# The sample tile projected from unsplit f32 weights in two column groups, with the splits of the output weights begun a quarter sooner

## The reference, cut to what matters

```python
y = jnp.concatenate([o_gla * silu(gg), o_pool * silu(pg), o_fox * silu(fg)], axis=-1) @ wo
return h + rmsnorm(y, post)
```

## Time and profile before

| | |
|---|---|
| median of 3 runs | 701.57 us (701.45 to 702.39) |
| the profiled execution, own time | 700.78 us |
| its span | 699.1 us |
| TensorE busy | 658.0 us, 94% |
| VectorE, ScalarE, GpSimd busy | 56%, 37%, 20% |

### The profile page before, as it was taken

How to read it: one execution, slowest core, us unless ns; L and a number is a source line. 1 busy time by engine, 2 the same in 40 slices (tenths; PEclk the granted TensorE clock), 3 DMA queues, 4 the chain that set the end, 5 groups by cost and what they waited for, 6 DMA issues and landing times.

```text
span 699.1 us, 13106 instructions
## 1 busy us (share of the span) xinstructions
PE 658.0 (94%) x5120; PEld 565.0 (81%) x5120; DVE 393.3 (56%) x706; ACT 262.1 (37%) x480; POOL 142.9 (20%) x162
## 2 busy tenths in 40 slices
PE   2999999999999999999999989989999997999996
PEld 2799999898999889999999955766576655688885
DVE  4824926672455305169999965444433559345543
ACT  6637344111111346122121155645574566231321
POOL 4034112111111011233312040222222103112210
PEclk9999999999999999999999999999999999999999
DMA  8411103131100032352210381667676512033232
GB/s 248 124 38 49 43 1 75 29 94 31 32 26 8 4 84 97 98 166 77 61 31 1 119 272 42 179 180 209 186 226 176 207 37 100 9 98 106 75 122 90
DMA packets 60759, 67.29 MB, mean 96 GB/s; under 512 B 15188, under 2 KB 50907, under 8 KB 60697
## 3 DMA queue, kind: packets, MB, share of 16 engines
q1 hardware_dynamic: 55529, 51.37, 24.9%
q0 software_dynamic: 5168, 15.08, 7.3%
HBM read 57.71 MB, written 8.68 MB: 95 GB/s over the span
## 4 chain that ended last, share of the span: by engine, by line
PE 82%; DVE 9%; ACT 4%; issue 2%; SPq 1%; DMA 1%; DVEq 0%
PE PS L1764 14%; PE PS L1765 13%; PE PS L1766 13%; PE PS L1693 5%; PE PS L1692 5%; PE PS L1694 5%; PE PS L2053 3%; PE PS L2035 3%; PE PS L1988 3%; PE PS L2010 2%; PE PS L1953 2%; PE PS L1940 2%; DVE rows_odd L1576 2%; DVE YF L1455 1%; DVE wol_a L1598 1%
## 5 line engine op out<-in xcount | busy, mean ns | idle before, releaser
L1764 PE MATMUL PS<-xh,wh 128*128 128x368 f32 x576 | 196.1, 340 | 0.3 <-DVE RA L1392 0.3
L1765 PE MATMUL PS<-xl,wh 128*128 128x368 f32 x576 | 190.2, 330 | 0.0
L1766 PE MATMUL PS<-xh,wl 128*128 128x368 f32 x576 | 189.8, 329 | 0.0
L582 POOL TENSOR_TENSOR wl<-wr,wh 128x1024 fp32r<-128x1024 f32 x24 | 61.5, 2560 | 292.0 <-ACT wh L944 291.7
L1764 PEld LDWEIGHTS PS<-xh,wh 128*128 128x128 f32 x576 | 108.2, 188 | 4.4 <-issue 1.8
L1765 PEld LDWEIGHTS PS<-xl,wh 128*128 128x128 f32 x576 | 108.2, 188 | 0.9
L1766 PEld LDWEIGHTS PS<-xh,wl 128*128 128x128 f32 x576 | 108.2, 188 | 0.0
L1264 DVE TENSOR_TENSOR wr<-wr,small 128x1024 f32<-128x1024 f32 (+1 forms) x26 | 37.1, 1426 | 43.3 <-DMA wr<-in_w_in_dram 43.2
L1692 PE MATMUL PS<-woh,yh 128*128 128x512 f32 (+1 forms) x144 | 56.1, 390 | 0.6 <-DVE wol_b L1598 0.6
L1435 DVE RECIPROCAL RA<-RA 128x1104 f32<-128x1104 f32 x8 | 56.4, 7053 | 0.3
L1694 PE MATMUL PS<-woh,yl 128*128 128x512 f32 (+1 forms) x144 | 56.0, 389 | 0.0
(11 more groups left out here) (305 smaller groups left out, 1084.2 us busy)
## 6 DMA issues: line engine op xcount, KB each, us to landing
wr<-in_w_in_dram SPq DMA_DIRECT2D x24, 512.0 KB, 3.7
kpage<-in_cache_fox_k_dram SPq DMA_DIRECT2D x64, 192.0 KB, 2.7
RA<-in_cache_fox_v_dram POOLq DMA_DIRECT2D x32, 192.0 KB, 3.7
pagesB<-in_cache_fox_v_dram POOLq DMA_DIRECT2D x32, 192.0 KB, 3.6
YF<-in_x_prompt_dram SPq DMA_DIRECT2D x8, 512.0 KB, 6.8
xres<-in_x_prompt_dram SPq DMA_DIRECT2D x8, 512.0 KB, 3.9
out_y_p_dram<-zout SPq DMA_DIRECT2D x16, 256.0 KB, 2.1
wo_raw_a<-in_w_out_dram SPq DMA_DIRECT2D x6, 512.0 KB, 4.8
```

The lines of the kernel that those rows point to most:

```text
L582: eng.tensor_tensor(low, wr[:, c % 2, :, 0:m], wh[:, c % 2, :, 0:m].bitcast(F32), ALU.subtract).then_inc(wlo_done, 1)
L1764: pe.matmul(out, high, xh[:, k, cols], start=(k == 0), stop=False)
L1765: pe.matmul(out, high, xl[:, k, cols], start=False, stop=False)
L1766: ins = pe.matmul(out, low, xh[:, k, cols], start=False, stop=(k == KT - 1))
```

## The change

Five edits, which go together:

- The sample tile is projected from the unsplit weights with plain f32 matmuls: for each k-block two matmuls of 64 stationary columns and 512 moving ones, the first into PSUM partitions 0 to 63 of the slot's first bank, the second into partitions 64 to 127 of its second bank. 16 matmuls in place of 48. Its Y is no longer split (one piece of work less for ScalarE and for GpSimd).
- The raw blocks 0 to 5 must live longer, so the low parts 0 to 5 have a place of their own, over `QK`, which is free once the last scores are made. Blocks 6 and 7 are still overwritten by their low parts: the sample tile uses them first, and VectorE's X 6 waits for that (`sample_late`).
- In the order, the sample tile moves from behind the last sum to behind the products of (2,3,0) and (2,3,1), and its "E" to behind the turned tile (2,3,4), ahead of the last product and sum.
- W 0 to 2 move from the quarter (2,2) to (2,1), and the others follow sooner; `wo_high(0)` waits for the keys of the last sequence to be used instead of its values, `wo_high(3)` for its turned probabilities. X 0 to 3 stand together behind the exponentials of (2,2).
- `rooms` is 2 for the quarter (2,2): all scores of the last quarter are made in its first part, and both "M" of tiles 6 and 7 stand in its second.

```diff
-        rooms = max(1, len(units) - 1 - after)
+        rooms = 2 if (p, q) == (2, 2) else max(1, len(units) - 1 - after)
...
-TAIL = {(2, 2, 0): [("W", 0), ("W", 1)], (2, 2, 1): [("X", 0), ("W", 2)],
-        (2, 2, 2): [("X", 1), ("X", 2), ("W", 3)], (2, 2, 3): [("X", 3), ("W", 4), ("Y", SAMPLE)],
-        (2, 3, 0): [("X", 4), ("W", 5), ("Y", FIRST)], (2, 3, 1): [("X", 5)], (2, 3, 2): [("W", 6)],
-        (2, 3, 3): [("X", 6), ("W", 7)], (2, 3, 4): [("X", 7)]}
+TAIL = {(2, 1, 1): [("W", 0), ("W", 1), ("W", 2)], (2, 2, 1): [("W", 3), ("W", 4), ("W", 5)],
+        (2, 2, 3): [("X", 0), ("X", 1), ("X", 2), ("X", 3)], (2, 3, 1): [("X", 4), ("X", 5), ("W", 6), ("Y", FIRST)],
+        (2, 3, 3): [("W", 7), ("S", SAMPLE), ("X", 6), ("X", 7)], (2, 3, 4): [("E", SAMPLE)]}
...
+        def out_part(user, half):
+            r = slice(NS * half, NS * half + NS) if user[1] == NTILE else slice(0, P)
+            return s_head(user, half)[r, :]
...
             def wo_high(k):
                 if k == 0:
-                    drained(act, ("s_attend", NB - 1))
+                    drained(act, ("s_scores", NB - 1, 2))
+                elif k == 3:
+                    drained(act, ("s_probsT", NB - 1, 1))
...
             def wo_low(k):
+                if k == 0:
+                    s_ready(dve, P1S[-1])
+                elif k == 6:
+                    dve.wait_ge(sample_late, 1)
                 dve.wait_ge(wohi_done, k + 1)
...
             def project_out(user):
                 t = user[1]
                 s_taken(pe, user)
+                if t == NTILE:
+                    drained(pe, ("s_outT", NB - 1))
+                    late_first = [6, 7, 0, 1, 2, 3, 4, 5]
+                    for k in late_first:
+                        pe.wait_ge(d_wo[k], 16)
+                        y = Y[:, k, ycol(t):ycol(t) + NS]
+                        lower = pe.matmul(out_part(user, 0), y, wo_raw[k][:, 0:D // 2], start=(k == 6),
+                                          stop=(k == 5), skip_group_check=True)
+                        upper = pe.matmul(out_part(user, 1), y, wo_raw[k][:, D // 2:D], start=(k == 6),
+                                          stop=(k == 5), skip_group_check=True)
+                        if k == 7:
+                            upper.then_inc(sample_late, 1)
+                    lower.then_inc(out_half, 1)
+                    upper.then_inc(s_full, 1)
+                    return
```

More of the change, by code:

```diff
@@ L216, in plan @@
     order += [("V", unit) for unit in behind] + [("R", ("sum",) + behind[0][:2])]
-    for n, t in enumerate(PROJ):
+    for n, t in enumerate(PROJ[1:], 1):
         if n >= 2:
-            order.append(("Y", ("proj", t)))
-        if n:
-            order.append(("E", ("proj", PROJ[n - 1])))
+            order += [("Y", ("proj", t)), ("E", ("proj", PROJ[n - 1]))]
         order.append(("S", ("proj", t)))
@@ L243, in slot_of @@
     return SF[user] % 2
+OUT_USERS = [k for k in SUSERS if k[0] == "proj"]
+OUT_OF_SLOT = {k: sum(slot_of(o) == slot_of(k) for o in OUT_USERS[:i + 1]) for i, k in enumerate(OUT_USERS)}
 P1S = [k for k in SUSERS if k[0] == "P1"]
@@ L261, in sem, with stage @@
             return ctx.enter_context(nc.semaphore(name))
+        def stage(*tensors):
+            with ExitStack() as s:
+                return [s.enter_context(nc.sbuf_tensor(n, d, t)) for n, d, t in tensors]
+        _, wol_a = stage(("pad_y", [P, 8 * NT], F32), ("wol_a", [P, 6, D], F32R))
         YF = sb("YF", [P, 14 * NT])
@@ L306, in build @@
         PS = ctx.enter_context(nc.psum_tensor("PS", [P, 8, 512], F32))
-        def stage(*tensors):
-            with ExitStack() as s:
-                return [s.enter_context(nc.sbuf_tensor(n, d, t)) for n, d, t in tensors]
         region_a = ("RA", [P, 6 * NT], F32)
@@ L322, in build @@
             ("rows_odd", [P, 2 * (score_width(6) + score_width(7))], F32))
-        wol_a, _, yh0, yl0, yh1, yl1, xres, zout, woh, wol_b, gpost = stage(
-            ("wol_a", [P, 6, D], F32R), ("pad_a", [P, 6 * NT - 6 * D], F32),
-            ("yh0", [P, KT, P], F32R), ("yl0", [P, KT, P], F32R), ("yh1", [P, KT, P], F32R),
+        _, yh0, yl0, yh1, yl1, xres, zout, woh, wol_b, gpost = stage(
+            ("pad_a", [P, 6 * NT], F32), ("yh0", [P, KT, P], F32R), ("yl0", [P, KT, P], F32R), ("yh1", [P, KT, P], F32R),
             ("yl1", [P, KT, P], F32R), ("xres", [P, D], F32), ("zout", [P, D], F32),
@@ L429, in build @@
         out_half, half_squared = sem("out_half"), sem("half_squared")
+        sample_late = sem("sample_late")
         def place(key):
@@ L495, in s_emptied @@
         def s_emptied(eng, user):
-            eng.wait_ge(s_free[slot_of(user)], PROJ.index(user[1]) // 2 + 1)
+            eng.wait_ge(s_free[slot_of(user)], OUT_OF_SLOT[user])
         def s_ready(eng, user):
@@ L887, in _ @@
                     load_bias(2)
-            for n_, t in enumerate(PROJ):
+            for n_, t in enumerate(PROJ[1:]):
                 g.wait_ge(yhi_done, n_ + 1)
-                m = P if t < NTILE else NS
-                g.tensor_tensor(yl[n_ % 2][:, :, 0:m], Y[:, :, ycol(t):ycol(t) + m], yh[n_ % 2][:, :, 0:m].bitcast(F32),
+                g.tensor_tensor(yl[n_ % 2][:, :, :], Y[:, :, ycol(t):ycol(t) + P], yh[n_ % 2][:, :, :].bitcast(F32),
                                 ALU.subtract).then_inc(ylo_done, 1)
@@ L1140, in squares_out @@
                     act.wait_ge(d_y, 32 * n_)
-                act.activation(zout[0:m, low], s_slot(user)[0:m, low], ACT.Square, accum_out=zhalf[0:m, 0:1]
+                act.activation(zout[0:m, low], out_part(user, 0), ACT.Square, accum_out=zhalf[0:m, 0:1]
                                ).then_inc(half_squared, 1)
@@ L1145, in squares_out @@
                 s_ready(act, user)
-                act.activation(zout[0:m, high], s_slot(user)[0:m, high], ACT.Square, accum_out=zstat[0:m, 0:1]
+                act.activation(zout[0:m, high], out_part(user, 1), ACT.Square, accum_out=zstat[0:m, 0:1]
                                ).then_inc(half_squared, 1)
@@ L1161, in y_high @@
             def y_high(n_):
[L1163 to L1168, removed]
+                t = PROJ[1 + n_]
+                drained(act, ("sum", 2, t // 2))
                 if n_ >= 2:
-                    s_ready(act, ("proj", PROJ[n_ - 2]))
-                act.activation(yh[n_ % 2][:, :, 0:m], Y[:, :, ycol(t):ycol(t) + m], ACT.Copy).then_inc(yhi_done, 1)
+                    s_ready(act, ("proj", PROJ[n_ - 1]))
+                act.activation(yh[n_ % 2][:, :, :], Y[:, :, ycol(t):ycol(t) + P], ACT.Copy).then_inc(yhi_done, 1)
             for kind, key in PLAN:
                 if kind == "Y":
-                    y_high(PROJ.index(key[1]))
+                    y_high(PROJ.index(key[1]) - 1)
                 elif kind == "W":
@@ L1609, in finish @@
                     dve.wait_ge(half_squared, 2 * n_ + n_half + 1)
-                    ins = dve.tensor_tensor(zout[0:m, cols], s_slot(user)[0:m, cols], gpost[0:m, cols], ALU.mult)
+                    r = slice(NS, 2 * NS) if t == NTILE and n_half else slice(0, m)
+                    ins = dve.tensor_tensor(zout[0:m, cols], out_part(user, n_half), gpost[r, cols], ALU.mult)
                 ins.then_inc(s_free[slot_of(user)], 1)
@@ L2080, in project_out @@
                     cols = slice(512 * half, 512 * half + 512)
-                    ins = product(out[0:m, cols], lambda k: (yh[n_ % 2][:, k, 0:m], yl[n_ % 2][:, k, 0:m]),
+                    ins = product(out[:, cols], lambda k: (yh[n_ % 2][:, k, :], yl[n_ % 2][:, k, :]),
                                   lambda k: (woh[:, k, cols], wol[k][:, cols]))
```

3 lines of the change are left out of this document (1 added, 2 removed).

## The result

**The times.** The changed kernel takes 697.29 us, the median of eight executions (696.65 to 699.66), against 702.37 us (701.35 to 704.55), the median of eight of the kernel before: ratio 0.9931, 95% interval 0.9915 to 0.9947. That is 0.69% faster, some 4.8 us. The forecast was 696.8 us, within 695.6 to 699.4. Its profiled execution has an own time of 696.65 us and a span of 695.0.

The account below looks back on a forecast made before the run. TensorE, busy 94% of the span, was taken as the bound, with idle time at 560 to 605. First full tile at 600.1 instead of 604.93 gives -4.8 us against the median 701.57: 696.8 us, range 695.6 to 699.4.

Parts of the forecast that it names:

- The sum: Whole kernel: first full tile at 600.1 instead of 604.93, so span and time fall by 4.8 us.
- A, the sample tile: Sample tile's projection on TensorE: eight f32 pairs at 0.90 us take 7.2 us instead of 11.11, -3.9 us.
- B, three early high parts: ScalarE's queue at (2,1): W 0 to 2 delay the cached values to 564.86, +1.1 us of TensorE idle.
- C, the last scores: Quarter (2,2): tile's maximum at 576.7 instead of 578.78; TensorE waits 0.5 us for exponentials instead of 2.41.
- D, VectorE: Low parts and copies: X 0 to 3 until 584.35, copy until 586.5 (+0.7); products of (2,3) start at 587.5 as before.
- E, the hand-over: Values to first full tile: sample tile until 596.6, new wait for its PSUM slot, first full tile at 600.1, -4.8 us.
- The step that was wrong: Eight full tiles after the sample tile: no gap, so the end moves by as much as the first full tile.
- rival 1: Tail: clock falls to 1.2 GHz over values and sample tile, +1.7 us, 698.5; chance 0.13.
- rivals 2 and 3: Sample tile's f32 pairs: groups don't overlap, 704.0 us, chance 0.04; or weight loads show, 701.0 us, chance 0.03.
- rival 4: ScalarE: the early high parts' 2.94 us passes on whole instead of 1.1, +1.8 us, 698.6; chance 0.10.

Follow-up runs that it names:

- one_group: The changed kernel with both halves of the sample tile in PSUM partitions 0 to 63, one column group: 703.74 us, ratio 1.0022 to the kernel before.
- w_late: The changed kernel with high parts W 0 to 2 moved back to quarter (2,2), beside W 3 to 5: 698.00 us, ratio 0.9932 to the kernel before.
- before_qk: The kernel before with only low parts 0 to 5 placed over QK and X 0 moved right ahead of X 1: 703.59 us, ratio 1.0017.
- rooms_old_2: The changed kernel with the old spreading of the last scores (rooms as before), run again for a second profile: 702.02 us, once.
- x0_early: The changed kernel with X 0 alone moved ahead of VectorE's copy of (2,2,3): 696.44 us, ratio 0.9912 to the kernel before.
- rooms_old: The changed kernel with the old spreading of the last scores (rooms as before): 701.44 us, ratio 0.9970 to the kernel before.
- again_before: The kernel before, unchanged, run once more for a second profile: 700.80 us, once.

## Why the prediction was right

By its own steps. Positions are those of after's own profile, whose head is 0.43 us longer than the one that the forecast counted from. So where a position up to the sample tile agrees with the forecast as it stands, it came 0.43 us sooner than forecast when counted from R, and the close agreement is in part luck:

- **The sum.** Forecast -4.8 us, and the ratio gives -4.8. Between the profiles it is -5.76 to the first full tile, +1.2 in the full tiles, +0.43 in the head, -4.1 in all. The forecast was 0.93 too cautious up to the first full tile (it had 604.93 - 600.1 = 4.83): 0.43 ahead of the sample tile, 0.23 in it and 0.27 behind it. And it was blind to the 1.2 behind. The two misses nearly cancel, so the total is better than its parts, by luck.
- **A, the sample tile.** 7.2 us forecast, 6.97 measured (589.40 to 596.37): a pair of f32 matmuls costs 0.86 us, nearly the bound by the slope alone (0.86 = 512 x 1.68 ns). The 40 ns beside the slope, read from smaller sizes, doesn't show at 512 columns. The overlap of column groups was taken from the earlier trace rows, and one_group shows that it is what the 6.97 rests on. The Trainium skill's rule (TensorE: Matmul & The Clock Gate, "Packing small matmuls") that weight loads are hidden only between different row groups does not show here: both groups use all rows, and a record's 0.43 us is 512 columns at 0.84 ns, half the slope of 1.68 ns a column for two records, which leaves no room for a load. In after's timeline the next loads (0.14 us each) start at 589.40 and 589.41, beside the matmuls that start then.
- **B, three early high parts.** Forecast +1.1, measured +0.81 (w_late). The order on ScalarE was as forecast, but records overlap a little: from the first copy behind W (564.01) to the cached values (564.97) it took 0.96 us, not the 1.1 of the durations added up (the copies start at 564.01, 564.28 and 564.41), and W was done 0.18 sooner, counted from R.
- **C, the last scores.** The last maximum was forecast for 576.7 and came at 576.73, the wait for exponentials was forecast at 0.5 and is 0.67.
- **D, VectorE.** X 0 to 3 were forecast at 579.45 to 584.35 and ran from 579.74 to 584.37; the turned tile's copy ended at 586.55, forecast 586.5. X 4 and 5 ended at 590.4, forecast 590.6, and nobody waited. The transposes at 2.4 GHz took 1.09 us and the products began at 587.62, forecast 587.5.
- **E, the hand-over.** 599.60, forecast 600.1, with the new wait for the slot where it was put, at 0.21 us. SAMPLE's end to the first full tile took 3.23 us, forecast 3.5.
- **The step that was wrong**, though the total came right: "the other eight tiles follow without a gap, so what moves the first full tile moves the end by as much". There is no gap, but a step is 2.8 ns longer on average since the low parts 0 to 5 lie elsewhere (before_qk), which takes back 1.1 us; the other 0.1 of the 1.2 is the first matmul behind the wait for the slot.
- **The rivals.** The clock did not fall in the tail in either profile of after (rival 1), and the two idle pieces named there came out as 1.56 and 1.57 us instead of 1.9 and 1.75; rooms_old_2 shows how near it was, since it fell there with the wait for VectorE 0.3 us longer and that for the exponentials 0.5 us longer. Groups without overlap and visible weight loads (rivals 2 and 3) are refuted by the 0.43 us steps. ScalarE passed on less than forecast, not more (rival 4).

By stretches, of the 5.76 us:

- **The sample tile itself** gives 11.11 - 6.97 = 4.14.
- **The order** gives 1.20. What stands between the values of (2,3,0) and (2,3,1) and the first full tile, the sample tile left out, took 593.82 - 589.39 = 4.43 us before, with waits of 0.62 us for VectorE's copy and 0.57 for X 7. After, it takes 599.60 - 596.37 = 3.23: the sample tile runs while VectorE makes these, and only the 0.21 for the slot is left. No run undoes the order alone; this is read from the two timelines.
- **Ahead of them**, from R to the end of those values, 0.42 is left (26.41 before, 25.99 after). The scores ahead bring 0.59, or 2.2 with the clock that they keep up. The early high parts take 0.81, and X 0 standing behind the copy instead of ahead of it takes 1.14 (x0_early). What the sample's Y brings by not being split was not tried apart.

Rows of the kernel before that the second item rests on, in TensorE's timeline:

```profile
589.39 0.44 PE L2035 MATMUL PS<-ident,rows_odd 128*128 128x128 f32 x2
...
591.46 1.30 PE L2053 MATMUL PS<-PT,VR 128*64 128x256 f32 x12 [0.62 <-DVE PT L1632]
```

What stays open: why the place of the low parts changes the pace, and why it does so in matmuls that don't read them. And what makes the clock hold in some executions of rooms_old and fall in others, with the same waits to 0.01 us.

## What to carry to other kernels

With 64 stationary columns, two plain f32 matmuls in two column groups cost here what one costs (0.86 us at 512 columns), and beat six fp32r products (1.38); check it by their starts in the timeline, since without the groups the same edit loses. Work that is ready belongs where the engine would otherwise wait: putting the sample tile there gave 1.2 us. Compare profiles from a mark just ahead of the change: executions here scatter by 3 us, distances from the mark by 0.02 as long as the clock does the same behind it. Of edits that "go together", undo each alone: here one cost 0.8 us for nothing, one low part stood 1.1 us from its best place, and one that seems worth half a microsecond in one profile is worth 2.2 in another.

## What the runs showed of the hardware

- **The place of moving operands changes the pace of a stream of matmuls, a little.** The same 384 fp32r matmuls of 512 columns step at 0.2286 us with six of the eight low parts in one region of SBUF, and at 0.2314 in another, with 0.2319 and 0.2322 after shifts of 32 and 1920 bytes there. That is 1.1 to 1.4 us of 87.5. The k-blocks whose low parts were not moved slow down as much as the others (0.681 to 0.690 us for three matmuls), so it isn't a cost of reading the moved operand alone.
- **The clock can fall behind idle pieces shorter than the 2.41 us of before, and need not.** With pieces of 1.18 and 1.87 us it held in one profile and fell in the next, from 2.4 to 1.2 GHz for some 3.4 us. With 0.67 and 1.57 us it held in all six profiles taken, and behind 2.41 or 2.42 us it fell in all three (before, again_before, before_qk). It falls at other places too, where no edit was made.
- **VectorE beside GpSimd.** Of the two low parts X 4 and X 5, the one that started while GpSimd made its own took 2.84 us in after (3.40 before), where the median of the six is 1.22 and four alone took 4.63. In after it was hidden.
